# Attention steps in a new order, with three buffers of probabilities in turn

## What is computed

```python
def row(r):                          # neighbourhood attention, layer 0
    s_lat = einsum(q_r, k_blk) * scale + bias      # 8 rows x 16 columns around each query
    s_ctx = einsum(q_r, kc) * scale                # 256 context keys
    p = softmax(concatenate([s_lat, s_ctx]))
    return einsum(p_lat, v_blk) + einsum(p_ctx, vc)
...
def block(n):                        # sliding window, layer 1
    s_lat = where(ok, einsum(q_b, k_w) * scale, NEG)
    p = softmax(concatenate([s_lat, s_ctx, s_sink]))
    return einsum(p[..., :span], v_w) + einsum(p[..., span:span + n_ctx], vc)
```

## Time and profile before

| | us |
|---|---|
| median of 3 runs | 1729.92 |
| lowest, highest | 1725.09, 1729.98 |
| profiled execution | 1730.58 |
| its span | 1728.8 |
| attention of layer 0 | 334 to 790 |
| attention of layer 1 | 1374 to 1587 |

### The profile page before, as it was taken

One profiled execution on the slowest core, in us unless ns is written; L12 is line 12 of the kernel. 1 busy time (PEld: TensorE's weight loads), 2 busy tenths in 40 slices (PEclk: granted clock), 3 DMA queues, 4 the chain that ended last, 5 costly groups with the idle time before them and its releaser, 6 DMA issues.

```text
span 1728.8 us, 25991 instructions
## 1 busy us (share of the span) xinstructions
PE 1623.0 (94%) x10106; PEld 1025.1 (59%) x10106; DVE 672.5 (39%) x1537; ACT 548.8 (32%) x1253; POOL 36.8 (2%) x108
## 2 busy tenths in 40 slices
PE   6999999899999999889999899999999799999995
PEld 4676866556565556544747666665564355555484
DVE  2123444413323214331245643234354255554265
ACT  0242242323323224332022332124214355554023
POOL 0000000000000000000000000000000011111000
PEclk9999999899999999999999999999999899999997
DMA  9100021112123113000445411000001000001353
GB/s 381 57 25 25 2 98 62 62 62 104 44 74 123 47 40 123 25 13 28 157 167 155 174 46 52 13 25 25 13 1 49 25 13 1 25 14 43 107 182 107
DMA packets 41145, 120.63 MB, mean 70 GB/s; under 512 B 4288, under 2 KB 14784, under 8 KB 39744
## 3 DMA queue, kind: packets, MB, share of 16 engines
q1 hardware_dynamic: 41024, 118.97, 19.7%
HBM read 109.52 MB, written 9.44 MB: 69 GB/s over the span
## 4 chain that ended last, share of the span: by engine, by line
PE 74%; issue 16%; DVE 5%; ACT 3%; DMA 2%; POOL 0%; SPq 0%; DVEq 0%; ACTq 0%; POOLq 0%
PE proj L990 22%; PE mixed L990 13%; PE scores L990 5%; PE proj L974 5%; PE mixed L974 4%; PE mixed L1110 3%; PE turned L1096 3%; PE scores L1208 2%; PE scores L1076 2%; PE scores L1236 2%; PE scores L1079 1%; ACT vstage L1679 1%; PE turned L1247 1%; PE mixed L935 1%; PE turned L935 1%
## 5 line engine op out<-in xcount | busy, mean ns | idle before, releaser
L990 PE MATMUL proj<-hT,weights 128*128 128x512 f32 (+1 forms) x1264 | 512.5, 552 | 10.2 <-DVE yT L1358 3.6
L990 PEld LDWEIGHTS proj<-hT,weights 128*128 128x128 f32 x1264 | 234.3, 194 | 215.5 <-issue 205.0
L990 PE MATMUL mixed<-hT,weights 128*128 128x512 f32 (+1 forms) x336 | 146.8, 580 | 0.8 <-ACT pair L1679 0.8
L990 PE MATMUL mixed<-yT,weights 128*128 128x256 f32 (+1 forms) x432 | 122.7, 442 | 0.0
L1679 ACT ACTIVATE work<-work,stat 128x640 f32<-128x640 f32 (+8 forms) x144 | 108.8, 755 | 42.7 <-DVE stat L1417 38.9
L1516 DVE SCALAR_TENSOR_TENSOR work<-work,turned 128x128 f32<-128x128 f32 (+1 forms) x152 | 53.0, 349 | 142.1 <-PE turned L1247 138.9
L1679 ACT ACTIVATE work<-turned 128x512 f32<-128x512 f32 (+2 forms) x136 | 72.8, 535 | 109.7 <-PE turned L1092 98.2
L1096 PEld LDWEIGHTS turned<-consts,work 128*128 128x128 f32 (+4 forms) x656 | 74.9, 140 | 54.8 <-issue 34.3
L1096 PE MATMUL turned<-consts,work 128*128 128x128 f32 (+4 forms) x656 | 99.8, 279 | 7.8 <-ACT work L1679 7.8
L990 PEld LDWEIGHTS mixed<-yT,weights 128*128 128x128 f32 x432 | 82.1, 190 | 38.9 <-issue 31.1
L990 PEld LDWEIGHTS mixed<-hT,weights 128*128 128x128 f32 x336 | 62.8, 193 | 63.5 <-issue 61.3
(11 more groups left out here) (252 smaller groups left out, 2127.5 us busy)
## 6 DMA issues: line engine op xcount, KB each, us to landing
weights<-in_weights SPq DMA_DIRECT2D x138, 512.0 KB, 3.7
tables<-in_bias SPq DMA_DIRECT2D x8, 1281.0 KB, 7.2
hT<-in_xT SPq DMA_DIRECT2D x8, 640.0 KB, 16.0
yT<-in_weights SPq DMA_DIRECT2D x8, 512.0 KB, 8.4
work<-in_xT SPq DMA_DIRECT2D x24, 128.0 KB, 3.6
x1T<-yT SPq DMA_DIRECT2D x12, 256.0 KB, 2.2
work<-in_weights SPq DMA_DIRECT2D x4, 512.0 KB, 16.8
pair<-in_weights SPq DMA_DIRECT2D x4, 512.0 KB, 17.6
```

The costliest lines, as they stand in the source:

```text
L990: last = nc.tensor.matmul(PJ[BANK_OF[u]][:, 0:n], weights[:, w % WBUFS, k, :], src[:, k, t0:t0 + n], start=(k == 0), stop=(k == KT - 1))
```

## The change

Three things. A third buffer for probabilities: `kvT` in layer 0, the key part of pair slot 0 in layer 1, both unused then; units take the three in turn, so VectorE waits for the turn of unit x-3. The softmax step is split into top (VectorE's maxima) and exp (ScalarE's exponentials), and a step of the pipeline is now: scores of x+2, transpose 0 of x, top of x+2, transpose 1, exp of x+2, a gap, transpose 2, pv of x-1. And `alternate` and `interleave` place filler only in such gaps, one a step, as many units or quarters as are due.

```diff
-    slots, passed, done, out = sum(s[0] != "softmax" for s in main), 0, 0, []
+    marked = any(s[0] == "gap" for s in main)
+    slots, passed, done, out = sum(not marked or s[0] == "gap" for s in main), 0, 0, []
     for s in main:
-        out.append(s)
-        passed += s[0] != "softmax"
+        if s[0] != "gap":
+            out.append(s)
+        passed += not marked or s[0] == "gap"
...
-        step += turns[:2]
-        if x + 2 < n:
-            step.append(("scores", *named(x + 2)))
-        step += turns[2:]
-        if x + 2 < n:
-            step.append(("softmax", *named(x + 2)))
+        new = named(x + 2) if x + 2 < n else None
+        if new:
+            step.append(("scores", *new))
+        step += turns[:1]
+        if new:
+            step.append(("top", *new))
+        step += turns[1:2]
+        if new:
+            step.append(("exp", *new))
+        step += [("gap",)] + turns[2:]
...
+        def prob(uid, hh):
+            buffers = (work[:, 0:1280], work[:, 1280:2560], pk(0) if uid[1] else kvT[:, :])
+            return buffers[number(uid) % 3][:, hh * 640:(hh + 1) * 640]
...
-                    if before(uid, 2):
-                        dve.wait_ge(*at(("turned", before(uid, 2), turned_by(before(uid, 2), hh))))
+                    if before(uid, 3):
+                        dve.wait_ge(*at(("turned", before(uid, 3), turned_by(before(uid, 3), hh))))
```

More of the change, by code:

```diff
@@ L488, in before, with number @@
     return None if i < 0 else ("att", l, i // N_UNITS[l], i % N_UNITS[l])
+def number(uid):
+    return uid[2] * N_UNITS[uid[1]] + uid[3]
 def turn_banks():
@@ L610, in att_slot @@
             return pair_slot(("sw" if l else "na", j))[0]
-        prob = [[work[:, (2 * x + h) * 640:(2 * x + h + 1) * 640] for h in range(2)] for x in range(2)]
+        def prob(uid, hh):
+            buffers = (work[:, 0:1280], work[:, 1280:2560], pk(0) if uid[1] else kvT[:, :])
+            return buffers[number(uid) % 3][:, hh * 640:(hh + 1) * 640]
         prob_t = [work[:, 2560 + x * 1408:2560 + (x + 1) * 1408] for x in range(2)]
@@ L1095, in s_ptrans @@
                     pe.wait_ge(*at(("softmax_act", uid, hh)))
-                    last = nc.tensor.transpose(to[0:w, :], prob[uid[3] % 2][hh][:, o:o + w], ident)
+                    last = nc.tensor.transpose(to[0:w, :], prob(uid, hh)[:, o:o + w], ident)
                 done(last, ("turned", uid, g))
@@ L1402, in s_vgather, with s_top @@
                      ("proj_free", u), *([("filled", "na", j, "v")] if 4 * g + 4 >= VG else []))
-            def s_softmax(uid, unit):
+            def s_top(uid, unit):
                 _, l, j, i = uid
-                st = stat[:, i % 4, :]
+                st = stat[:, number(uid) % 4, :]
                 dve.wait_ge(*at(("scores", uid)))
@@ L1661, in _ @@
                     "modulate": s_modulate, "mm": s_mm,
-                    "rope": s_rope, "vgather": s_vgather, "softmax": s_softmax, "ptrans": s_ptrans, "pv": s_pv,
+                    "rope": s_rope, "vgather": s_vgather, "top": s_top, "ptrans": s_ptrans, "pv": s_pv,
                     "gate0": s_gate0, "lin_scale": s_lin_scale, "lin_mul": s_lin_mul,
@@ L1773, in s_mm, with s_exp @@
                         scale=QSCALE if scaled else 1.0)
-            def s_softmax(uid, unit):
+            def s_exp(uid, unit):
                 _, l, j, i = uid
-                st, (_, n) = stat[:, i % 4, :], unit_cols(unit)
+                st, (_, n) = stat[:, number(uid) % 4, :], unit_cols(unit)
                 for hh in range(2):
@@ L1781, in s_softmax @@
                         run(st[:, 4 + hh:5 + hh], col("sink", j + 4 * hh), ACT.Exp, bias=st[:, hh:hh + 1])
-                    pr = prob[i % 2][hh][:, 0:n]
+                    pr = prob(uid, hh)[:, 0:n]
                     run(pr, pr, ACT.Exp, [("softmax_act", uid, hh)], scale=-1.0, bias=st[:, hh:hh + 1],
@@ L1926, in s_ptrans @@
                     pool.wait_ge(*at(("turned", two_back, len(turn_groups(unit_of(two_back))) - 1)))
-                sums = stat[:, uid[3] % 4, 6:8].unsqueeze(2).broadcast_to([P, 2, DH])
+                sums = stat[:, number(uid) % 4, 6:8].unsqueeze(2).broadcast_to([P, 2, DH])
                 pool.tensor_copy(sums_wide[uid[3] % 2].rearrange("p (h n) -> p h n", h=2), sums).then_inc(
```

4 lines of the change are left out of this document (2 added, 2 removed).

## The result

| | before | after |
|---|---|---|
| median, us | 1727.55 (4 runs) | 1738.17 (4 runs) |
| lowest, highest | 1725.09, 1729.98 | 1735.76, 1739.93 |
| profiled span | 1728.8 | 1737.1 |
| mean granted clock, profiled | 0.980 | 0.984 |

The changed kernel is slower by 0.57% (ratio 1.0057, 95% interval 1.0041 to 1.0073), 10.6 us. The forecast was slower, and right in that; its time, 1756, was 18 us too long, and the measured one lies just under its range. A median here is over all runs of a kernel, while a ratio leaves out a single run far above the others (1776.6 us of e3, 1987.4 us of e9).

What follows compares the result with a forecast made beforehand. TensorE's work plus the moments in which it stands was taken as the bound. Profiled 1730.6 us, plus 21.8 of waits (14.3 layer 0, 7.5 layer 1) and 4 of clock, gave 1756.4, so 1756 us; range 1740 to 1778.

Steps and rivals of the forecast that it cites:

- bank waits of layer 0: Layer 0 attention: filler units behind one another in one PSUM bank make TensorE wait for its emptying, 39.3 us.
- other waits of layer 0: Layer 0 attention: waits at the first scores, one gap without a product and the last two units, 3.7 us.
- all waits of layer 1: Layer 1 attention: new rope waits, first and second scores, rope chains and the last head pair, 19.2 us.
- boundaries between kinds: TensorE in attention: 0.1 us per change of product kind, a few fewer of them, taken as 0 to -3 us.
- clock: Gathering steps: a third at half clock loses 6 us, two old falls go; +4 us, bounds -10 and +30.
- the rope chains: Layer 1, three new head pairs: of 1.4 us waiting on the rope chain 0.85 us remain, 2.6 us in all.
- the ends: Layer 1, last head pair: transposes wait for ScalarE's two exponentials, about 4 us as before.
- Rival 1: Attention: bank empties sooner, each of 42 new waits costs 0.3 us; faster, 1717 us; chance 0.07.
- rival 2: Attention: no difference, mean wait price near 0.65 us or clock gives 15 us back; 1730 us; chance 0.05.
- Rival 5: Attention: old waits stay as something else releases the maxima, half of 27 us not given back; 1769 us; chance 0.08.
- rival 4: Gathering steps: they stay at 1.2 GHz nearly throughout, +23 us over the forecast; 1775 us; chance 0.11.
- Rival 3: Attention: long uninterrupted runs of products keep 2.4 GHz, falls vanish, -11 us; 1741 us; chance 0.08.

Runs made afterwards that it cites:

- e3: The changed kernel with a second place for filler in each step, behind the values; 1732.1 us, ratio 1.0025 to the kernel before.
- e9: e7 with maxima and exponentials queued directly behind the scores, ahead of the filler, TensorE's order unchanged; 1796.1 us, ratio 1.0391 to the kernel before.
- e1: The changed kernel with its new steps and three buffers, but filler strewn as before in both layers; 1750.8 us, ratio 1.0140 to the kernel before.
- e7: The changed kernel with the old order of steps, keeping three buffers and one place for filler; 1809.8 us, ratio 1.0476 to the kernel before.
- e6: The changed kernel with layer 1's rope products moved apart from their own products; 1734.8 us, ratio 1.0050 to the kernel before.
- e8: The changed kernel with the edits of e5 (layer 0) and e6 (layer 1) together; 1727.3 us, ratio 1.0004 to the kernel before.
- e10: e8 with each head pair's last query quarter and its rope product one step earlier in layer 1; 1721.1 us, ratio 0.9963 to the kernel before.
- e5: The changed kernel with a second place for filler in layer 0, between the first two groups of transposes; 1730.1 us, ratio 1.0007 to the kernel before.

## Why the prediction was right in sign and wrong in size

With the means of both pairs of profiles: idle 105.3 to 127.0 us, +21.7. Busy time fell by 10.8 us, from 1620.6 to 1609.8. The sum behind "work" splits this: in attention 625.4 to 620.0, -5.4 us, and in the rest of the program 968.7 to 967.1, -1.6 us, which I take as chance, since no order changed there and two executions of before differ by 3.6 us. What the low clock added fell by 5.0 us in attention and rose by 1.3 us outside. Together +10.9, as the spans have it (1725.9 to 1736.8).

| term | forecast | measured |
|---|---|---|
| bank waits of layer 0 | 39.3 | 35.1 |
| other waits of layer 0 | 3.7 | 6.1 |
| all waits of layer 1 | 19.2 | 17.7 in the rows |
| waits less those of before | +21.8 | +21.7 |
| boundaries between kinds | 0 (0 to -3) | -5.4 in attention |
| clock | +4 (-10 to +30) | -3.7 |
| work outside attention | 0 | -1.6 (chance) |

**The waits were right, nearly one by one.** For the first head pair I had 0.7, 1.0, 0.7, 1.7, 0.7, 1.9, 2.0, 1.9, 1.3, 1.3 us, in order; the trace shows 0.61, 0.84, 0.61, 1.54, 0.62, 1.74, 1.88, 1.69, 1.13, 1.17, each 6 to 16% less. Each price came from counting what stood ahead of the emptying in one engine's queue. The old waits for the maxima are gone as said, and those for POOL but for 1.8 us. The other waits of layer 0 are 2.4 us over the forecast, since transposes still wait 3.9 us for ScalarE. So the forecast was a little high on the bank and on layer 1 and a little low here, and that +21.8 met +21.7 is in part luck (within attention it is +21.0, the rest outside). Layer 1's rope products measured 6.8 us (forecast 6.2), the products behind them 3.4 (4.4), the rope chains 2.6 (2.6), and the ends 3.3 (4.0). Rival 1 asked for prices under 0.65 us and the mean is 0.95 (35.1 us in 37 waits); rival 2 falls with it. Rival 5 wanted half of the old 27 us to stay, and the maxima's went entirely. One figure of the rivals doesn't add up: rival 4's +23 us over 1756 is 1779 and not 1775. And the 0.45 in the clock's sum has no row behind it.

**Two steps failed. The first is the one on boundaries:** "a boundary between kinds of product costs 0.1 us and there are a few fewer, which I take as 0 to -3 us". It is the one term that came out beyond its own bounds. Fewer they are, but not a few. I had counted waits in the new order and not the places. Between transposes stand 22 of 122 places before and 59 of 73 after. Places apart fell from 100 to 14.

At full clock the traces show these intervals, start to start. From a 512 wide product matmul to the next matmul it is 0.43 us, be it its own kind or a transpose, and 0.52 us to scores or values. A product entered from transposes starts after 0.11 us, from values after 0.20, from scores after 0.31 to 0.40 by their width. The same gate product shows the exit: 446.41 - 442.85 = 3.56 us from its start to transposes (e1), 446.49 - 442.83 = 3.66 us to values (e7).

But transposes followed by scores or values take 0.20 instead of 0.11 us too, so most places pay this with or without filler in between. What filler itself adds lies at its entry: from the first matmul of a 512 wide product to its second it is 0.43 us where transposes stand before the product, and 0.53 us where scores or values do (medians; the same in each of five traces: before, after, e1, e3, e7). A product that had to wait for the bank has a longer first interval too, 0.50 us on the mean. Over attention these longer first intervals add up to 6.1 us before and 2.7 us after: 3.4 of the 5.4 us. Another 1.0 us are waits that the profile books as work. A transposing matmul is shown as busy for 0.27 us (mean 279 ns below), while the next one can start after 0.11; where the next one waits, the 0.16 us between count as busy.

```profile
L1112 PE MATMUL turned<-consts,work 128*128 128x128 f32 (+3 forms) x448 | 65.9, 279 | 4.1 <-ACT work L1695 3.9
```

There is no one price for a place apart: 5.4 us for 86 places between before and after, 6.0 for 58 (e1), 9.4 for 48 (e3, its share of the 10.7 us within attention) and 12.7 for 58 (e7), so 0.06 to 0.22 us. Of e3's 9.4 us, 2.9 are first intervals and 3.7 are waits booked as work, as 29 transposes wait there and 7 after. Some 3 us of it, and 1 us of the 5.4, stay open.

**The second is the clock, which had the wrong sign.** It is the larger miss: +4 us against -3.7. I let a third of the gathering steps, 25 us, run at half clock; the clock rows have 6.8 us there. Windows of these steps, and of the places of the earlier trace rows, after (start and end, length, busy, clock, DMA share, GB/s):

```profile
415.00:425.00 10.00, 8.12 (x74) 0.86 0.14 52
425.00:435.00 10.00, 7.18 (x64) 0.97 0.64 252
435.00:445.00 10.00, 8.83 (x84) 1.00 0.55 222
...
670.00:680.00 10.00, 7.42 (x50) 0.83 0.80 313
...
728.00:732.00 4.00, 4.00 (x39) 1.00 0.00 0
...
752.00:756.00 4.00, 4.00 (x24) 1.00 0.03 13
```

There are two short falls, of 3.4 us each, at 422 and at 675 us. From 425 to 435 us TensorE was busy for only 7.2 of 10 us, with a mean grant of 0.97. The falls at 728 and 752 us went, as I had said. The mean grant of the whole run is 0.977 to 0.982 in the 50 runs of before beside the experiments, and 0.984 to 0.986 in the four after: the sign is sure. The size is not. e6, e8 and e10 have layer 0 in the order of after or of e5, which had 12.9 and 12.7 us at 1.2 GHz there, and show 3.7 to 4.1 us. Rival 3 named the direction, with 1741 us the nearest of all figures. That it came so near is luck: it had the clock give back 11 us and the boundaries nothing, and the fall near 334 us is still there. The rule beside it (the Trainium skill, Perfetto Trace Analysis, Matmul Optimizations: matmuls back to back in batches) has the traces with it here by 0.005 of the mean grant. Strewing the same work (e1) gave 0.975. But one place for filler in the old order gave 0.974 (e7), so batches of filler alone don't bring the clock. The rule that speaks against sharing a bank (the Trainium skill, Perfetto Trace Analysis, Optimizing Tensor Performance) is borne out too: 35 us in layer 0.

**The starting point** cost some of the rest. I built on a median of three runs of 1729.9 us; the later medians of the same kernel are 1727.1 to 1727.8. Of the 18 us that the forecast was too long, 5.4 are boundaries, 7.7 the clock, 1.6 the chance outside attention and 2.4 the start; about 1 is rounding and the difference between the profiled executions and the medians.

## What to carry to other kernels

Count not only what each wait costs but at how many places the kind of work on TensorE changes, and put filler between two pieces where it lengthens nothing, here two groups of transposes. Gathering the filler in one place pays for its bank waits only in part. A second such place took 22 of the 36 waits between units and 9 us of idle time away and left the busy time as it was (e5). Place the filler by what its emptying is queued ahead of: strewn, it made the transposes of layer 0 wait 20.2 us for ScalarE and POOL instead of 5.7 (e1). And try an order of steps together with its place for filler: one place cost 72 us more with the old steps than with the new (e7), half of it idle time and half work and clock.

## What the runs showed of the hardware

A change of kind has a price on TensorE that depends on the kinds. It is none between 512 wide products and transposes, and 0.09 us from either to scores or values. Behind scores or values a 512 wide product's first interval is 0.53 instead of 0.43 us. A transpose is shown as busy for 0.27 us and can be followed after 0.11, so a wait behind one is 0.16 us longer than the idle time that the profile shows. The granted clock differs with the order of the same work, from 0.974 (e7) to 0.988 (e10), and the longest idle goes with the lowest clock only roughly: e9 has e7's idle and 0.978.
